# Small decay products by 32-key squares and a fused row maximum in the first mixer of a three-layer block kernel

## The reference, cut to what matters

```
# branch 1: attention over selected keys, 4 heads of 128
s = einsum(q, ks) * HEAD_DIM ** -0.5
s = where(valid, s, -inf)
p = softmax(s)                        # needs the row maximum
# branch 2: gated linear attention, 4 heads, 64 decay channels, values of 128
b     = cumsum(log_gate)
diff  = b[t] - b[s]
decay = exp(where(causal, diff, -inf))
att   = einsum('bthd,bshd,bhtsd->bhts', q, k, decay)
o     = o_inter + einsum('bhts,bshe->bhte', att, v)
```

## Time and profile before

| | us |
|---|---|
| median of 3 runs (lowest, highest) | 970.76 (970.74, 971.71) |
| the profiled execution's own time | 971.24 |
| its span (first to last instruction) | 969.4 |
| PE busy | 959.2 (99%) |
| DVE busy | 619.6 (64%) |
| ACT busy | 549.6 (57%) |
| mean granted clock of TensorE | 1.000 of 2.4 GHz |

### The profile page before, as it was taken

How to read it: one execution, slowest core, us unless ns; L and a number is a source line. 1 busy time by engine, 2 the same in 40 slices (tenths; PEclk the granted TensorE clock), 3 DMA queues, 4 the chain that set the end, 5 groups by cost and what they waited for, 6 DMA issues and landing times.

```text
span 969.4 us, 14020 instructions
## 1 busy us (share of the span) xinstructions
PE 959.2 (99%) x5770; PEld 851.4 (88%) x5770; DVE 619.6 (64%) x935; ACT 549.6 (57%) x786; POOL 130.1 (13%) x43
## 2 busy tenths in 40 slices
PE   9999999999999999999999999999999999999997
PEld 7888888888888888888888888899999999999886
DVE  4997957777322666747777322376548689888643
ACT  7676346666433567847665433644454687666442
POOL 0011041000665000020000766200000000000000
PEclk9999999999999999999999999999999999999999
DMA  8654225555555453344455455364443535555441
GB/s 294 226 180 168 88 88 176 202 187 180 193 192 190 161 214 130 134 171 176 174 206 186 174 197 194 142 218 160 163 156 131 217 132 195 187 196 184 176 172 44
DMA packets 25232, 168.46 MB, mean 174 GB/s; under 512 B 2816, under 2 KB 3776, under 8 KB 5328
## 3 DMA queue, kind: packets, MB, share of 16 engines
q1 hardware_dynamic: 25024, 167.49, 48.0%
q10 hardware_dynamic: 144, 0.07, 0.0%
HBM read 166.50 MB, written 1.05 MB: 173 GB/s over the span
## 4 chain that ended last, share of the span: by engine, by line
PE 84%; DVE 7%; ACT 5%; issue 2%; DMA 1%; SPq 0%; DVEq 0%; ACTq 0%
PE bank L681 20%; PE bank L683 20%; PE bank L682 20%; PE bank L763 12%; PE bank L767 6%; DVE wlo L1845 3%; ACT whi L1233 3%; PE bank L709 1%; DVE a L2059 1%; DMA raw<-w_stream 1%; ACT b L1709 1%; PE bank L900 0%; PE bank L817 0%; PE bank L1013 0%; DVE b L2339 0%
## 5 line engine op out<-in xcount | busy, mean ns | idle before, releaser
L1845 DVE TENSOR_TENSOR wlo<-raw,whi 128x2048 fp32r<-128x2048 f32 (+2 forms) x152 | 310.7, 2044 | 253.7 <-ACT whi L1233 253.7
L1233 ACT ACTIVATE whi<-raw 128x2048 fp32r<-128x2048 f32 (+1 forms) x154 | 293.1, 1905 | 150.8 <-PE bank L683 148.3
L2577 POOL TENSOR_TENSOR wlo<-raw,whi 128x1024 fp32r<-128x1024 f32 (+1 forms) x37 | 129.1, 3491 | 486.3 <-ACT whi L1233 479.0
L763 PE MATMUL bank<-nhl,whi 128*128 128x512 f32 x512 | 124.2, 392 | 0.0
L763 PEld LDWEIGHTS bank<-nhl,whi 128*128 128x128 f32 x512 | 93.9, 188 | 19.1 <-issue 0.7
L681 PE MATMUL bank<-mhi,whi 128*128 128x258 f32 x384 | 108.6, 283 | 0.0
L682 PE MATMUL bank<-mlo,whi 128*128 128x258 f32 x384 | 108.3, 282 | 0.0
L683 PE MATMUL bank<-mhi,wlo 128*128 128x258 f32 x384 | 108.2, 282 | 0.0
L681 PE MATMUL bank<-nhl,whi 128*128 128x258 f32 (+3 forms) x320 | 92.5, 289 | 0.0
L682 PE MATMUL bank<-nhl,whi 128*128 128x258 f32 (+3 forms) x320 | 91.2, 285 | 0.0
L683 PE MATMUL bank<-nhl,wlo 128*128 128x258 f32 (+3 forms) x320 | 90.4, 283 | 0.0
(11 more groups left out here) (317 smaller groups left out, 1755.0 us busy)
## 6 DMA issues: line engine op xcount, KB each, us to landing
raw<-w_stream SPq DMA_DIRECT2D x154, 1024.0 KB, 4.8
cst<-consts SPq DMA_DIRECT2D x1, 1088.0 KB, 6.9
h<-x_rows SPq DMA_DIRECT2D x4, 256.0 KB, 5.3
raw<-w_stream SPq DMA_DIRECT2D x2, 512.0 KB, 6.9
out_rows<-e SPq DMA_DIRECT2D x3, 256.0 KB, 2.0
e<-g_post SPq DMA_DIRECT2D x1, 512.0 KB, 3.2
raw<-w_stream SPq DMA_DIRECT2D x1, 352.0 KB, 10.1
vec<-vectors SPq DMA_DIRECT2D x1, 258.5 KB, 9.0
```

The lines of the kernel that those rows point to most:

```text
L763: return pe.matmul(us[c].t[:, :], w[:, k, c * P:c * P + P].hi, nboth[:, k, :], start=k == 0, stop=k == 7)
L1233: act.activation(whi[j][:, 0:n], raw[j][:, 0:n], ACT.Copy).then_inc(s_hi.up(i))
L1845: dve.tensor_tensor(wlo[j][:, 0:m], raw[j][:, 0:m], whi[j][:, 0:m].bitcast(F32), ALU.subtract).then_inc(s_lod.up(i))
L2577: pool.tensor_tensor(wlo[j][:, m:n], raw[j][:, m:n], whi[j][:, m:n].bitcast(F32), ALU.subtract).then_inc(s_lop.up(i))
```

## The change

It has four edits.

1. The level products. For one unit, `gla_1` on PE now issues 28 products instead of 8. Each writes only a small rectangle of the PSUM tile: levels 4 to 7 in four squares of 32 keys by 32 queries along the diagonal, level 3 in four rectangles 16x16, level 2 in two 32x32, level 1 in two of 32 keys by 64 queries. A square that begins at key 32·j is written to PSUM partitions from 32·j on. Levels 1 to 4 share one 128x128 part of the bank, levels 5, 6 and 7 (the last with the diagonal) have one each: one bank in place of two.
2. The masked copies. `gmask` has four masks of 128 columns in place of eight; DVE's `gla_1` has four copies, into one tile (128x128, 128x64, 128x64, 128x128), each behind the one before, and no addition. That tile is what PE's `gla_2` reads.
3. The last level. At l = 7 only the keys are scaled: one subtraction fewer, and of the two multiplications one becomes a plain copy.
4. The row maximum. DVE's `att_1` has two `tensor_tensor_reduce` (one for each query half) that add the mask, multiply by minus the scale and take the minimum, in place of the addition, the two maxima and the scaling. ACT's exponential takes scale -1, and for the second query half waits for the second of them.

```diff
-                for half in range(2):
-                    u = begin("gl", n, half)
-                    for i in range(4):
-                        l = half * 4 + i + 1
...
-                        x = pe.matmul(u.t[:, i * P:i * P + P], kx, qx, start=True, stop=True)
+                squares = [slice(b, b + 32) for b in range(0, P, 32)]
+                on.wait_ge(*s_lvq.at(4, 1))
+                for b in squares:
+                    pe.matmul(u.t[b, b], *level(4, b, b), start=True, stop=True)
+                for b in squares:
+                    before, after = slice(b.start, b.start + 16), slice(b.start + 16, b.stop)
+                    pe.matmul(u.t[before, after], *level(3, before, after), start=True, stop=True)
+                for before, after in ((squares[0], squares[1]), (squares[2], squares[3])):
+                    pe.matmul(u.t[before, after], *level(2, before, after), start=True, stop=True)
+                for before in squares[0:2]:
+                    pe.matmul(u.t[before, 64:P], *level(1, before, slice(64, P)), start=True, stop=True)
+                for l in (5, 6):
+                    on.wait_ge(*s_lvq.at(l, 1))
+                    for b in squares:
+                        pe.matmul(u.t[b, (l - 4) * P + b.start:(l - 4) * P + b.stop], *level(l, b, b), start=True, stop=True)
+
+                on.wait_ge(*s_lvq.at(7, 1))
+                for b in squares:
+                    o = u.t[b, 3 * P + b.start:3 * P + b.stop]
+                    pe.matmul(o[:, 0:32:2], k0[:, b], q0[:, b][:, 0:32:2], start=True, stop=True)
+                    x = pe.matmul(o[:, 1:32:2], QKE[lo:lo + 64, 7, c + b.start:c + b.stop], q0[:, b][:, 1:32:2], start=True, stop=True)
+                x.then_inc(u.full)
...
-                on.wait_ge(*s_am.at(n))
+                on.wait_ge(*use["gl", n].gone())
...
+                dve.copy_predicated(am, gm[:, 0:P], u.t[:, 0:P]).then_inc(own.up())
+                for i, hs in ((1, 4), (2, 2)):
+                    s = slice(i * P, i * P + P)
+                    on.wait_ge(*own.last())
+                    dve.copy_predicated(later_half(am, hs), later_half(gm[:, s], hs), later_half(u.t[:, s], hs)).then_inc(own.up())
+                on.wait_ge(*own.last())
+                dve.copy_predicated(am, gm[:, 3 * P:4 * P], u.t[:, 3 * P:4 * P]).then_inc(u.free)
...
-                dve.tensor_tensor(y, u.t[:, 0:3 * P], SEL, ALU.add).then_inc(u.free)
-                on.wait_ge(*u.gone())
                 for tt in range(2):
-                    dve.tensor_reduce(mx[:, tt:tt + 1], y[:, KEYS_OF[tt]], AX.X, ALU.max).then_inc(own.up())
-                on.wait_ge(*own.last())
-                dve.tensor_scalar(mx, mx, -scale, None, ALU.mult).then_inc(s_nmx.up(hd))
+                    s = KEYS_OF[tt]
+                    dve.tensor_tensor_reduce(out=y[:, s], in0=u.t[:, s], in1=SEL[:, s], scale=-scale, scalar=3.0e38, op0=ALU.add, op1=ALU.min,
+                                             accum_out=mx[:, tt:tt + 1]).then_inc(u.free if tt else s_nmx.up(hd))
```

More of the change, by code:

```diff
@@ L40 @@
     ("ones", 128), ("cosA", 32), ("sinA", 32), ("cosI", 16), ("sinI", 16),
[L41 removed]
+    ("inval", 512), ("gmask", 512), ("smask", 384), ("dftc", 256),
 ]
@@ L94, in constants @@
         masks.append((s // (2 * hs) == t // (2 * hs)) & (s % (2 * hs) < hs) & (t % (2 * hs) >= hs))
-    masks.append(s == t)
-    put("gmask", np.stack(masks, 1).astype(np.float32))
+    put("gmask", np.stack([sum(masks[0:4]), masks[4], masks[5], masks[6] | (s == t)], 1).astype(np.float32))
     tri = np.where(s < t, 0.0, BIGNEG).astype(np.float32)
@@ L337, in plan_banks @@
     proj(4, [("qkT", tt, j) for tt in range(2) for j in range(2)])
-    proj(5, [("gl", 0, 0), ("gl", 0, 1)])
+    proj(5, [("gl", 0)])
     for i in range(1, 9):
         if i < 8:
-            banks.take("gl", i, 0)
-            banks.take("gl", i, 1)
+            banks.take("gl", i)
             if i >= 4:
@@ L537, in block_kernel @@
         SSH = [SS[:, j * 3 * P:(j + 1) * 3 * P] for j in range(2)]
-        AMS = [SS[:, (6 + j) * P:(7 + j) * P] for j in range(2)]
+        AMS = [AM[:, j * P:(j + 1) * P] for j in range(2)]
         GL = A(256)
@@ L633, in block_kernel @@
             ("qk0", 2), ("ropei", 2), ("ikd", 4), ("bb", 2), ("ls", 1), ("bsum", 2)))
[L634 removed]
+        s_lvd, s_lve, s_lvq = sig("lvd", grid(8, 2)[:14] + [(7, 1)]), sig("lve", range(8)), sig("lvq", grid(8, 2))
         s_rl, s_sc = sig("rl", range(8)), sig("sc", grid(8, 2))
         s_qrs, s_qg = sig("qrs", grid(2, 2)), sig("qg", grid(2, 2))
[L637 removed]
+        s_am0, s_sel, s_ropea = sig("am0", [0]), sig("sel", range(2)), sig("ropea", range(2))
         s_sig, s_og = sig("sig", range(2)), sig("og", range(2))
@@ L923, in gla_1 @@
                 c = p * 256 + tt * P
-                for half in range(2):
-                    u = begin("gl", n, half)
-                    for i in range(4):
-                        l = half * 4 + i + 1
[L928 to L931, removed]
-                        x = pe.matmul(u.t[:, i * P:i * P + P], kx, qx, start=True, stop=True)
-                    x.then_inc(u.full)
+                q0, k0 = QK0[lo:lo + 64, 0, c:c + P], QK0[lo:lo + 64, 1, c:c + P]
@@ new lines, in gla_1, with level @@
+                u = begin("gl", n)
+                def level(l, keys, queries):
+                    return QKE[lo:lo + 64, l, c + keys.start:c + keys.stop], QKE[lo:lo + 64, l, c + queries.start:c + queries.stop]
+                squares = [slice(b, b + 32) for b in range(0, P, 32)]
[5 more added lines that the diff above has]
+                    pe.matmul(u.t[before, after], *level(3, before, after), start=True, stop=True)
@@ L1433, in att_1 @@
                 sm = small[:, 136 + 2 * hd:138 + 2 * hd]
-                on.wait_ge(*s_nmx.at(hd))
                 for tt in range(2):
+                    on.wait_ge(*(use["qk", hd].gone() if tt else s_nmx.at(hd)))
                     y = SSH[hd % 2][:, KEYS_OF[tt]]
-                    act.activation(y, y, ACT.Exp, bias=mx[:, tt:tt + 1], scale=scale,
+                    act.activation(y, y, ACT.Exp, bias=mx[:, tt:tt + 1], scale=-1.0,
                                    accum_out=sm[:, tt:tt + 1]).then_inc(s_prob.up(hd, tt))
@@ L1947, in level_scale @@
                 dv = DEs[l % 2].rearrange("p (b u s) -> p b u s", u=2, s=hs)
+                if l == 7:
+                    on.wait_ge(*use["qkb", 1].gone())
+                    dve.tensor_copy(QKE[:, l, 1:512:2], QK0[:, 1, 1:512:2]).then_inc(s_lvq.up(l, 0))
+                    on.wait_ge(*s_lve.at(l))
+                    dve.tensor_tensor(QKE[:, l, 0:512:2], QK0[:, 1, 0:512:2], dv[:, :, 0, :].rearrange("p b o -> p (b o)"), ALU.mult).then_inc(s_lvq.up(l, 1))
+                    return
                 on.wait_ge(*s_lve.at(l))
@@ L2040, in gla_1 @@
             def gla_1(n):
-                am = AM[:, n % 2 * 256:n % 2 * 256 + 256]
-                us = [use["gl", n, half] for half in range(2)]
+                am, u = AMS[n % 2], use["gl", n]
                 on.wait_ge(*s_am0.at(0))
@@ L2046, in gla_1 @@
                 on.wait_ge(*TR)
+                on.wait_ge(*u.done())
                 def later_half(x, hs):
[L2050 to L2062, removed]
-                            on.wait_ge(*own.last())
-                on.wait_ge(*us[0].gone())
-                on.wait_ge(*us[1].gone())
-                dve.tensor_tensor(AMS[n % 2], am[:, 0:P], am[:, P:256], ALU.add).then_inc(s_am.up(n))
+                    return x.rearrange("p (b u t) -> p b u t", u=2, t=hs)[:, :, 1, :]
+                dve.copy_predicated(am, gm[:, 0:P], u.t[:, 0:P]).then_inc(own.up())
[5 more added lines that the diff above has]
+                dve.copy_predicated(am, gm[:, 3 * P:4 * P], u.t[:, 3 * P:4 * P]).then_inc(u.free)
             def cat_lo(s, name, hd):
```

5 lines of the change are left out of this document (3 added, 2 removed).

## The result

| | before | after |
|---|---|---|
| median, us | 970.90 (970.74 to 971.71, 4 runs) | 963.09 (962.73 to 965.21, 4 runs) |
| the profiled execution: time, span | 971.24, 969.4 | 965.21, 963.4 |
| output projection begins | 127.54 | 121.49 |
| from unit 1's first product to there | 26.62 | 22.36 |

The ratio is 0.992, with an interval of 0.991 to 0.993: 7.8 us faster, where 3.1 were forecast. The profiled execution is the longest of the four.

The account below looks back on a forecast made before the run. PE was taken as the bound. Products -3.1, change of form +0.8 and waits -0.8 gave -3.1 us against the profiled 971.24, so 968.1, with the median put at 967.7; the range was 963.5 to 975.

Parts of the forecast that it names:

- What bounds the kernel before: Unit 1's level products to output projection: PE is the bound; relieving DVE alone returns at most PE's 0.8 us of waits.
- Level products on PE, r = 0.025: PE's small products: 0.025 us between record starts, a unit 1.59 us in place of 1.98, -3.1 us over eight units.
- The early product, +0.8: PE's gx behind the small products in units 4 to 7: the change of form costs 4 x 0.2 = +0.8 us.
- Masked copies 1.09: DVE's chain of four copies takes 1.09 us a unit in place of 1.80, 5.7 us of DVE in all.
- Row maximum 0.80: DVE's row maximum takes 0.80 us a head in place of 1.31 (bounds 0.55 and 1.31), 2.0 us of DVE.
- PE is the one bound and its waits vanish: In the loop, a DVE step falls from 3.77 to 2.6 us, below PE's 2.7 to 4; PE's waits give -0.8 us.
- Last level, constant, banks: nothing: Last level, smaller mask constant and one bank fewer give nothing; at most the 0.8 us already counted.
- Behind the loop: After the output projection begins, the earlier start carries on; weight tile 17 keeps 4.0 us of slack.
- Rival 3: More overlap of PE's small products, 0.8 us a unit, and DVE becomes the bound: 963.7 us; chance 0.10.
- Rival 4: The small products let the granted clock fall from 2.4 to 1.2 GHz in the stretch: 980 to 990 us; chance 0.03.

Follow-up runs that it names:

- e7: The kernel before with four masked copies a unit in place of eight (levels 2, 3, 6 and 7 left out, output changed): 969.98 us, ratio 0.9989.
- e2: The kernel before with the new row maximum (two tensor_tensor_reduce) alone: 970.03 us, ratio 0.9989.
- e3: The changed kernel with the same 28 products a unit sorted by key square: 967.81 us, ratio 0.9964.
- e4: The changed kernel with DVE's subtraction for weight tile 16, lo(16), moved to the end of the loop: 966.08 us.
- e5: The changed kernel with the constant gmask padded back to 1024 columns: 965.00 us, against 965.56 for the changed kernel beside it.
- e14: The changed kernel with the transfers of weight tiles 18 and 19 held back until PE has made unit 5's products: 963.08 us, ratio 0.992.
- e1: The changed kernel with the row maximum as before (addition, two maxima, scaling): 967.66 us, ratio 0.9964.
- e9: The changed kernel with DVE's subtraction for weight tile 16, lo(16), moved to step 3, behind the row maximum of head 2: 965.64 us.
- e12: The changed kernel with DVE's subtraction for weight tile 16 in four pieces of 512 columns, one in each of steps 4 to 7: 965.97 us.
- e6: The changed kernel with all 28 small products of a unit issued twice: 967.72 us, ratio 0.9967.

## Why the prediction was wrong, by its steps

- **What bounds the kernel before**: right. PE, with DVE worth 0.8 us: e7 gave 0.9, e2 1.1.
- **Level products on PE, r = 0.025**: this is the step that failed. It was a size, and its lower bound said so: "If our records, in four such groups, did the same", 0.8 us a unit. The unit takes 0.69. I took the value by width because each load must still come in, and let L1113 count only for "a little below it". e3 shows that the value near the width rule is about right for products that follow one another in one PSUM group (1.64, forecast 1.59), and that the order written here isn't of that kind: level by level over four squares, nearly each product goes to another group than the one before (its two records, and at level 7 its two products, stay in one). I priced the products and not their order. Eight units at 1.29 less are 10.3 us in place of 3.1.
- **The early product, +0.8**: nearly nothing. A unit takes 0.69 with the way over to gx behind it, and also where a product of 128 rows follows at once (e4's unit 2, 100.75 to 101.44). From gx of unit 7 to the next line it is 0.42 (118.45 to 118.87), 0.31 before (124.76 to 125.07): 0.1 a unit, not 0.2.
- **Masked copies 1.09**: 1.13. **Row maximum 0.80**: 0.55, the lower bound; the second pass isn't held up, and the small instructions advance the queue by nearly nothing.
- **"PE is the one bound and its waits vanish"**: wrong, as a result of the products. The waits went from 0.8 to 1.6. What is late next was named in no term: lo(16), in front of unit 1 on DVE.
- **Last level, constant, banks: nothing**: not shown. The constant may be worth about 0.5 us at the start of the program (e5 and the starts named there), for which the prediction had no term; the others weren't run alone.
- **Behind the loop**: right. The 6.05 us at the output projection are the 6.0 of the span.
- **The rivals.** Rival 3 happened in the main, and near its price: 0.8 us a unit, DVE next, 963.7. DVE didn't become the one bound, though: in e14, at full clock, PE waits 2.5 us in all. I gave it 0.10 with the argument that 112 loads and records must also be issued. That argument has something in it, the stop in unit 3, but it costs about 1 us and not the overlap. Rival 4 happened too, from another cause than its own: not the small products let the clock fall but the waits between them, and it cost 2 to 4 us, since it lasted 7 us and not the whole stretch. Its one row, 0.536 against 0.379, wasn't evidence for a clock: the trace shows 1.00 from 1 to 9 us too. The fall of the clock, in some executions, is why the median moved between 963.1 and 965.6 from one set of runs to the next. The range ended at 963.5, right below rival 3's own price, and so left its faster half out.

What stays open: how much of the 0.69 is load and how much stream; why the clock falls in one execution and not in the next behind the same wait, and why it doesn't in e14; what sets the time at which a block is asked for; whether the constant gave the 0.5 us at the start; and why e1 is 4.6 above the change's first median.

## What to carry to other kernels

Before pricing many small products by width, look which PSUM partitions follow one another in the program: in turn over four groups of 32 they cost 0.012 us a record here, square by square, with 12 to 16 records in a row in one group, 0.029. When an engine that was the bound gets quicker by a third, look what stood ahead of its partners' work under the old cover, here a 2.3 us subtraction of no urgency, since a wait of 1 us can cost 2 to 4 more in clock. Moving it is no gain by itself, though (e4, e9, e12): look for what stands behind it. A stretch of many short instructions needs its instruction blocks on time: move a large transfer that isn't needed yet out of it.

## What the runs showed of the hardware that was not expected

- 56 fp32 records of 64x16 to 64x64 with their loads in 0.69 us, 0.012 a record; in another order 1.64.
- Idle time put down to issue inside a run of small products, 0.63 to 1.75 us, behind PE's 1449th instruction in eight runs; in e6 four shorter ones (0.17 to 0.87), 254 to 256 instructions apart or twice that. PE goes on 2.0 to 2.8 us behind the start of a 16 KB packet. The stop of the eight runs is gone when the weight tile is held back, and the packet then comes more than 2 us sooner.
- One wait of 0.99 us between units of small products was followed by 6 to 7 us at a granted clock of 0.50, in some executions, and by a clock of 1.00 in others (e1, e5, e14); with work in the wait the mean clock was 0.998 or more in four of four executions.
- DVE's multiplication of two 128x512 tiles took 2.56 us in place of 0.69 while POOL subtracted beside it. The Trainium skill names the pair's port "an exclusive lock, not a bandwidth split" (SBUF — State Buffer, SBUF: two separate sides); here DVE's instruction ended 0.5 us behind POOL's (125.96 and 125.41).
- The row maximum of 128x384 with mask and scale in 0.55 us, in two passes over PSUM.
